# A diffusion block on one core: tokens turned early and kept in SBUF, and another order of the first loads

## The reference, cut to what matters

```python
mod   = silu(c)     @ ada_w[i] + ada_b[i]        # 2048 -> 6 * 2048
sh1, sc1, g1, sh2, sc2, g2 = split(mod, 6)
mod_c = silu(c_ctx) @ ada_w[i] + ada_b[i]
csh1, csc1, ... = split(mod_c, 6)
h  = rms_norm(x,   norm1_g[i]) * (1 + sc1)  + sh1
hc = rms_norm(ctx, norm1_g[i]) * (1 + csc1) + csh1
proj = h @ w_in[i]                               # and hc @ w_in[i][:, :N_QKV]
```

## Time and profile before

| | us |
|---|---|
| median of 3 runs | 1719.82 |
| the profiled execution | 1720.02 |
| its span | 1718.3 |
| TensorE busy in it | 1677.8 (98%) |
| VectorE busy | 1086.3 (63%) |
| ScalarE busy | 752.6 (44%) |
| chain that ended last: TensorE, DMA, VectorE | 94%, 3%, 1% |

### The profile page before, as it was taken

The page is one execution under the profiler, slowest core; times in us unless marked ns, Lnnn a source line. Parts: engine busy times, 40 slices in busy tenths (PEclk is TensorE's granted clock), DMA queues, the critical chain, the costliest instruction groups (busy, mean ns, idle before and its releaser), DMA issues.

```text
span 1718.3 us, 23725 instructions
## 1 busy us (share of the span) xinstructions
PE 1677.8 (98%) x8768; PEld 1371.5 (80%) x8768; DVE 1086.3 (63%) x1366; ACT 752.6 (44%) x962; POOL 108.6 (6%) x161
## 2 busy tenths in 40 slices
PE   4999999999999999999999999999999999999997
PEld 1568888888888678888888788888888888888886
DVE  1338787768887674554555666666666666655556
ACT  2233321623222664444444555555555555544444
POOL 0002222122121000000000000000000000000000
PEclk7999999999999999999999999999999999999999
DMA  9999888269896128566565566666666665655552
GB/s 353 386 387 347 298 296 297 79 215 328 259 321 200 52 90 271 191 189 191 192 234 195 148 190 190 188 191 188 191 187 191 185 184 188 202 195 194 191 193 83
DMA packets 161813, 371.47 MB, mean 216 GB/s; under 512 B 11671, under 2 KB 12423, under 8 KB 160598
## 3 DMA queue, kind: packets, MB, share of 16 engines
q1 hardware_dynamic: 140240, 291.65, 52.5%
q0 software_dynamic: 20144, 74.22, 12.7%
q10 hardware_dynamic: 1366, 4.74, 0.7%
HBM read 368.36 MB, written 2.21 MB: 216 GB/s over the span
## 4 chain that ended last, share of the span: by engine, by line
PE 94%; DMA 3%; DVE 1%; issue 0%; ACT 0%; SPq 0%; DVEq 0%; POOL 0%; ACTq 0%
PE ps L1885 21%; PE ps L1884 11%; PE ps L1899 10%; PE ps L1901 10%; PE ps L1900 10%; PE ps L2253 5%; PE ps L2252 5%; PE ps L2254 5%; PE ps L1811 4%; PE ps L1813 3%; PE ps L1812 3%; DMA raw<-in_ada_w 3%; PE ps L1882 1%; PE ps L1803 1%; PE ps L1968 1%; PE ps L1950 1%
## 5 line engine op out<-in xcount | busy, mean ns | idle before, releaser
L1147 DVE TENSOR_TENSOR w_lo<-raw,w_hi 128x1024 fp32r<-128x1024 f32 x480 | 584.5, 1223 | 419.7 <-ACT w_hi L680 419.2
L680 ACT CAST w_hi<-raw 128x1024 fp32r<-128x1024 f32 x480 | 503.4, 1050 | 763.3 <-PE ps L1885 271.2
L1885 PE MATMUL ps<-h2T,w_hi 128*128 128x512 f32 x1320 | 462.7, 394 | 0.0
L1884 PE MATMUL ps<-h2T,w_lo 128*128 128x256 f32 x1320 | 366.8, 278 | 0.0
L1885 PEld LDWEIGHTS ps<-h2T,w_hi 128*128 128x128 f32 x1320 | 247.8, 188 | 53.7
L1884 PEld LDWEIGHTS ps<-h2T,w_lo 128*128 128x128 f32 x1320 | 248.2, 188 | 3.9
L1899 PE MATMUL ps<-w_hi,hT 128*128 128x512 f32 x512 | 201.7, 394 | 0.0
L1901 PE MATMUL ps<-w_hi,hT 128*128 128x512 f32 x512 | 199.4, 389 | 0.0
L1900 PE MATMUL ps<-w_lo,hT 128*128 128x512 f32 x512 | 199.3, 389 | 0.0
L1222 DVE SCALAR_TENSOR_TENSOR ada_acc<-ada_raw,silu_c,ada_acc 128x512 f32<-128x512 f32 x240 | 179.9, 750 | 29.4 <-DMA ada_raw<-in_ada_w 14.1
L603 POOL DMA_DIRECT2D ada_raw<-in_ada_w x128 | 91.2, 712 | 381.5 <-DVE ada_acc L1222 226.4
(11 more groups left out here) (231 smaller groups left out, 1985.6 us busy)
## 6 DMA issues: line engine op xcount, KB each, us to landing
raw<-in_ffn_w_up SPq DMA_DIRECT2D x176, 512.0 KB, 3.8
raw<-in_w_in SPq DMA_DIRECT2D x152, 512.0 KB, 4.8
ada_raw<-in_ada_w POOLq DMA_DIRECT2D x128, 512.0 KB, 5.9
raw<-in_ffn_w_down SPq DMA_DIRECT2D x88, 512.0 KB, 4.3
raw<-in_ada_w SPq DMA_DIRECT2D x64, 512.0 KB, 10.4
raw<-in_w_out SPq DMA_DIRECT2D x32, 512.0 KB, 4.4
raw<-in_w_branch_a SPq DMA_DIRECT2D x16, 512.0 KB, 3.6
raw<-in_w_branch_b SPq DMA_DIRECT2D x16, 512.0 KB, 3.6
```

Source lines behind the costliest of these rows:

```text
L680: act.copy(w_hi[:, s % SPLIT_SLOTS, :], raw[:, s, :]).then_inc(hi_ready[s], 1)
L1147: dve.tensor_tensor(w_lo[:, s % SPLIT_SLOTS, :], raw[:, s, :], w_hi[:, s % SPLIT_SLOTS, :], ALU.subtract).then_inc(lo_ready[s], 1)
L1884: pe.matmul(ps[:, b + t, 0:SEQ], w_lo[:, row4(s), at], high(kc), start=False, stop=False)
L1885: return pe.matmul(o, w_hi[:, row4(s), at], both(kc), start=False, stop=(kc == KC - 1))
```

## The change

- SP requests units 0 and 1 first, and the identity, `c` and `c_ctx` behind them. ACT requests the tokens first and the eight small loads of parameter rows behind them.
- The tokens are turned in 16 parts: part n holds channels of two kc for the two tiles of one stream, parts 0 to 7 for `x`, 8 to 15 for `ctx`. They stand behind units 3 to 11 of the first quarter (`TURN_AFTER`), in four PSUM banks. VectorE copies 7 and ScalarE 9 of them into `turned`, which lies where the low part of `hT` will lie. The modulation reads `turned` and waits for all copies once.
- TensorE turns the parameter rows behind unit 6 of the first quarter instead of ahead of all units. `turn_mod(0)` stands behind unit 15 instead of behind unit 17.
- VectorE's list: lambda first, then the scaling of `x`, three copies of turned parts, the parameter rows, the scaling of `ctx`, the other four copies. ScalarE copies its nine parts behind the second stream's root.
- K0 to K5 are requested earlier by 3 or 4 units, most of their tiles stand up to 4 units earlier, and three tiles of K5 stand behind the last unit instead of two. A first tile of a K waits for each of its two channels by itself.
- Two semaphores (`ones_ready`, `lam_ready`) are gone.

```diff
-K_AFTER = (3, 10)
-K_TILES = {(0, 0): (1, 6), (0, 1): (1, 8), (0, 2): (1, 10), (0, 3): (1, 12),
-           (1, 0): (1, 13), (1, 1): (1, 15), (1, 2): (2, 1), (1, 3): (2, 3),
-           (2, 0): (2, 6), (2, 1): (2, 8), (2, 2): (2, 10), (2, 3): (2, 12),
-           (3, 0): (2, 13), (3, 1): (2, 15), (3, 2): (3, 1), (3, 3): (3, 3),
-           (4, 0): (3, 5), (4, 1): (3, 6), (4, 2): (3, 8), (4, 3): (3, 9),
-           (5, 0): (3, 11), (5, 1): (3, 12), (5, 2): (3, 15), (5, 3): (3, 15)}
+K_AFTER = (0, 6)
+K_TILES = {(0, 0): (1, 3), (0, 1): (1, 5), (0, 2): (1, 6), (0, 3): (1, 8),
+           (1, 0): (1, 10), (1, 1): (1, 12), (1, 2): (1, 15), (1, 3): (2, 1),
+           (2, 0): (2, 4), (2, 1): (2, 5), (2, 2): (2, 7), (2, 3): (2, 8),
+           (3, 0): (2, 10), (3, 1): (2, 12), (3, 2): (2, 15), (3, 3): (3, 1),
+           (4, 0): (3, 4), (4, 1): (3, 5), (4, 2): (3, 7), (4, 3): (3, 9),
+           (5, 0): (3, 11), (5, 1): (3, 15), (5, 2): (3, 15), (5, 3): (3, 15)}
+TURN_PARTS = KC
+TURN_BANKS = (7, 1, 6, 5)
+TURN_AFTER = {3: (0, 1), 4: (2, 3), 5: (4, 5), 6: (6,), 7: (7,), 8: (8, 9), 9: (10, 11), 10: (12, 13), 11: (14, 15)}
+TURNS_OF_VECTOR = (0, 1, 2, 8, 10, 12, 14)
+TURNS_OF_SCALAR = tuple(n for n in range(TURN_PARTS) if n not in TURNS_OF_VECTOR)
...
     hT = place("hT", lat, [P, 2, 2, KC, SEQ], F32R)
+    turned = place("turned", lat, [P, 2, 2, KC, SEQ])
...
+        def turned_part(n):
+            st, pair = divmod(n, KC // 2)
+            return turned[:, st, 1, 2 * pair:2 * pair + 2, :].rearrange("p k n -> p (k n)")
+        def part_kept(n):
+            if n in TURNS_OF_VECTOR:
+                return kept_by_vector, TURNS_OF_VECTOR.index(n) + 1
+            return kept_by_scalar, TURNS_OF_SCALAR.index(n) + 1
...
-            sp.dma_start(ident, constants[:, C_IDENT:C_IDENT + P]).then_inc(rows_landed, 16)
-            sp.dma_start(param_rows[0:16, 0, :], c.rearrange("a (k p) -> (a k) p", p=P)).then_inc(rows_landed, 16)
-            sp.dma_start(param_rows[16:32, 0, :], c_ctx.rearrange("(k p) -> k p", p=P)).then_inc(rows_landed, 16)
...
                     n = KC * q + kc
+                    if n == 2:
+                        sp.dma_start(ident, constants[:, C_IDENT:C_IDENT + P]).then_inc(rows_landed, 16)
+                        sp.dma_start(param_rows[0:16, 0, :], c.rearrange("a (k p) -> (a k) p", p=P))\
+                            .then_inc(rows_landed, 16)
+                        sp.dma_start(param_rows[16:32, 0, :], c_ctx.rearrange("(k p) -> k p", p=P))\
+                            .then_inc(rows_landed, 16)
...
+            act.dma_start(tokens[:, 0:TOK, :], x[0].rearrange("(t p) n -> p t n", p=P)).then_inc(tokens_landed, 16)
+            act.dma_start(tokens[:, TOK:2 * TOK, :], ctx[0].rearrange("(t p) n -> p t n", p=P))\
+                .then_inc(ctx_landed, 16)
             act.dma_start(param_rows[0:96, 1, :], by_row(ada_b)).then_inc(rows2_landed, 16)
...
-                act.wait_ge(tokens_turned, kc + 1)
+                if kc == 0:
+                    act.wait_ge(kept_by_vector, len(TURNS_OF_VECTOR))
+                    act.wait_ge(kept_by_scalar, len(TURNS_OF_SCALAR))
...
-                    act.activation(modulated[:, kc % 4, st, :], ps[:, turn_bank(kc), st * SEQ:(st + 1) * SEQ],
+                    act.activation(modulated[:, kc % 4, st, :], turned[:, st, 1, kc, :],
...
                 root1(st)
+            for n in TURNS_OF_SCALAR:
+                act.wait_ge(tokens_turned, n + 1)
+                act.copy(turned_part(n), ps[:, TURN_BANKS[n % 4], :]).then_inc(kept_by_scalar, 1)
...
+            def keep_turned(n):
+                dve.wait_ge(tokens_turned, n + 1)
+                dve.tensor_copy(turned_part(n), ps[:, TURN_BANKS[n % 4], :]).then_inc(kept_by_vector, 1)
...
             mean_square1(0)
             inverse_root1(0)
             norm_tokens(0)
             norm_tokens(1)
+            keep_turned(0)
+            keep_turned(1)
+            keep_turned(2)
+            dve.wait_ge(vecs_turned, 2)
...
             mean_square1(1)
             inverse_root1(1)
             norm_tokens(2)
             norm_tokens(3)
+            for n in TURNS_OF_VECTOR[3:]:
+                keep_turned(n)
...
+            def turn_tokens(n):
+                st, pair = divmod(n, KC // 2)
+                if pair == 0:
+                    pe.wait_ge(normed1, TOK * (st + 1))
+                if n >= 4:
+                    pe.wait_ge(*part_kept(n - 4))
+                for i in range(2):
+                    kc = 2 * pair + i
+                    for t in range(TOK):
+                        mm = pe.transpose(ps[:, TURN_BANKS[n % 4], (2 * i + t) * P:(2 * i + t + 1) * P],
+                                          tokens[:, 2 * st + t, kc * P:(kc + 1) * P], ident)
                 mm.then_inc(tokens_turned, 1)
...
             for _, q, kc in ADA_UNITS:
                 unit_ada(q, kc)
-                if (q, kc) == (1, 1):
-                    turn_mod(0)
+                if (q, kc) == (0, 6):
+                    turn_vectors()
+                if q == 0:
+                    for n in TURN_AFTER.get(kc, ()):
+                        turn_tokens(n)
+                    if kc == KC - 1:
+                        turn_mod(0)
...
-                        if (s, t) in ((1, 1), (3, 1), (5, 2)):
+                        if (s, t) in ((1, 2), (3, 2), (5, 1)):
                             turn_mod(q)
-                if kc == 14:
-                    turn_tokens(SHARE * q)
-                if q and kc in (2, 4, 5):
-                    turn_tokens(SHARE * (q - 1) + {2: 1, 4: 2, 5: 3}[kc])
-            turn_tokens(KC - 3)
```

More of the change, by code:

```diff
@@ L728, in _ @@
             act.dma_start(param_rows[2 * FF_TILES:2 * FF_TILES + 1, 5, :], diff_norm_g).then_inc(rows2_landed, 16)
[L729 to L732, removed]
+            act.wait_ge(start_dve, 1)
             warm_up(ACT.Exp)
@@ L1162, in step @@
                 dve.wait_ge(start_dve, steps)
-            dve.memset(ones[:], 1.0).then_inc(ones_ready, 1)
+            step(dve.memset(ones[:], 1.0))
             step(dve.memset(epsilon[:], EPS))
@@ L1278, in _ @@
             norm_tokens(1)
+            keep_turned(0)
+            keep_turned(1)
+            keep_turned(2)
+            dve.wait_ge(vecs_turned, 2)
+            dve.tensor_copy(vecs[:, 2 * KC:512], ps[:, 3, 2 * KC:512]).then_inc(vecs_ready, 1)
+            dve.tensor_copy(vecs[:, 512:513], ps[:, 2, 88:89]).then_inc(vecs_ready, 1)
+            dve.wait_ge(vecs_ready, 3)
+            dve.tensor_scalar(dng[:], vecs[:, V_DNG:V_DNG + 1], 1.0 - LAMBDA_INIT, None, ALU.mult)\
+                .then_inc(vecs_ready, 1)
             mean_square1(1)
@@ L1767, in _ @@
             pe.wait_ge(c_ready, 1)
-            pe.wait_ge(ones_ready, 1)
-            def turn_tokens(kc):
-                if kc == 0:
-                    pe.wait_ge(normed1, 2 * TOK)
-                if kc >= 2:
-                    pe.wait_ge(modulated_ready, 2 * (kc - 1))
-                if kc % SHARE == 1:
-                    pe.wait_ge(mod1_ready, kc // SHARE + 1)
-                for t in range(2 * TOK):
-                    mm = pe.transpose(ps[:, turn_bank(kc), t * P:(t + 1) * P], tokens[:, t, kc * P:(kc + 1) * P],
-                                      ident)
+            def turn_tokens(n):
[9 more added lines that the diff above has]
+                                          tokens[:, 2 * st + t, kc * P:(kc + 1) * P], ident)
                 mm.then_inc(tokens_turned, 1)
@@ L1786, in turn_mod @@
                 if q:
-                    pe.wait_ge(modulated_ready, 2 * SHARE * q)
+                    pe.wait_ge(mod1_ready, q)
+                else:
+                    pe.wait_ge(kept_by_vector, len(TURNS_OF_VECTOR))
+                    pe.wait_ge(kept_by_scalar, len(TURNS_OF_SCALAR))
                 rows = PIECE_AT[-1] + 2
@@ L1813, in products_k, with unit_k @@
                 return pe.matmul(o, w_lo[:, row4(slot), at], hT[:, :, 0, kc, :], start=False, stop=(kc == KC - 1))
-            def unit_k(s, slot, t, b):
+            def unit_k(s, slot, t, b, head=False):
                 for i in range(2):
+                    if head and t == 0:
+                        pe.wait_ge(hT_ready, 2 * s + i + 1)
                     mm = products_k(slot, t, b, 2 * s + i, i)
@@ L1823, in head_k, with turn_vectors @@
                 if t == 0:
-                    pe.wait_ge(hT_ready, 2 * s + 2)
                     take(0, s)
-                mm = unit_k(s, s, t, 0)
+                mm = unit_k(s, s, t, 0, head=True)
                 if t == TILES - 1:
                     mm.then_inc(used[s], 1)
-            pe.wait_ge(rows2_landed, 128)
-            pe.wait_ge(vecs_ready, 1)
-            pe.transpose(ps[:, 3, V_ADAB:V_ADAB + P], param_rows[:, 1, :], ident)
-            for tap in range(TAPS):
-                pe.transpose(ps[:, 3, V_CONV + 88 * tap:V_CONV + 88 * (tap + 1)], param_rows[0:88, 2 + tap, :],
-                             consts[0:88, 0:88])
```

(17 more changed lines are left out.)

15 lines of the change are left out of this document (3 added, 12 removed).

## The result

The changed kernel took 1725.67 us (median of 16 runs) against 1720.08 us: ratio 1.0031, 95% interval 1.0025 to 1.0038, 4.3 to 6.5 us slower. Forecast were 1718.7 us, 1716.2 to 1723.4. One of the 16 runs took 5002 us with TensorE slow throughout and happens to be the profiled one; the ratio leaves it out, and all that follows reads another execution of the same kernel (1726.59 us, span 1724.9), which is the experiment `after_again`.

A forecast was written before the change was run, and what follows sets the result against it. The head, ending when job 1 starts (131.87 us), was taken as bound by DMA transfer, with TensorE 1.77 us behind at u63. u63 0.4 earlier and 0.7 off the tail gave -1.1: 1718.7 us, range 1716.2 to 1723.4.

The forecast's parts named there:

- c behind two units: Head, SP's queue: at 4.9 us a unit beside tokens, u1 lands at 12.1 and c about 12.6.
- rival D: Head: tokens crowd out the units, c 3.0 us later, DMA loss 5.2; +1.9, 1721.7 us; chance 0.08.
- What hangs on c: Head, behind c's landing: units start at 14.5, ScalarE squares x from 16.5, x can be turned from 23.8.
- What that does to the loads: Head, unit loads: u12 frees u20's slot at 45.5, not 43.3, so the DMA loses 2.2 us; bounds 0 to 9.3.
- the budget: Head, unit loads: u19 lands at 45.2; u20 must be asked for some 1.9 us before that, by 43.3.
- B: Head, turning: clock stays at 1.2 GHz through the parts; every part low +6.0, 1725.8 us; chance 0.13.
- C: Tail: clock falls around u60 to u63, tiles behind u63 cost 1.4 to 2.4 us more; 1720.1 to 1721.1; chance 0.11.
- E: End of the head: TensorE is not freed, u63 still runs 1.77 us behind its landing; 1720.5 us; chance 0.02.
- The tail: From u63 to job 1: 0.7 us goes with the two parts there; bounds 0.4 to 1.5.
- The start of the DMA: Fifth and sixth us: large loads requested first fill 0.75 us of empty DMA time; 0.8 us won, bounds 0 and 1.2.
- lateness: At u63: the 1.77 us that TensorE stood behind its data go, since nine parts fewer lie in the middle.
- rival A: Head: the loads never starve; -0.8 - 1.77 - 0.7 = -3.3, 1716.5 us, or 1716.1 with the fuller start; chance 0.16.

The follow-up runs named there:

- tokens_2k: The changed kernel with x and ctx each loaded in four strips of 512 columns, so in 2 KB pieces: 1725.09 us, ratio 1.0042.
- c_first: The changed kernel with one edit undone, identity, c and c_ctx requested ahead of unit 0 again: 1717.59 us, ratio 0.9983.
- squares_first: The changed kernel with x squared and scaled ahead of the work on c: 1718.28 us, ratio 0.9992.
- c_first_again: The changed kernel with identity, c and c_ctx ahead of unit 0, run once more: 1716.30 us, ratio 0.9985.
- order_back: The changed kernel with both orders of loads as before (c ahead of units, parameter rows ahead of tokens), the turning still changed: 1719.36 us, ratio 0.9993.

## Why the prediction was wrong, step by step

**The step that failed is "c behind two units": "I take 4.9. Then u1 lands at 2.3 + 9.8 = 12.1 and c about 12.6".** It lies between a mean over u3 and u4 (5.45) and one over five units (4.4), and both mixed times: u0 and u1 of the kernel before had mostly landed before the tokens came, and u4 came as they ended: from 6 to 9 us ScalarE's queue carried 0.09 MB of rows, SyncE's 1.01. The one row wholly inside, u3's 6.4, stood in the text and was given to rival D. Measured: u0 landed at 11.47, 10.6 behind its request; u1 at 17.81, 6.3 later; c_ctx at 20.48, 2.7 behind u1 where 0.5 was allowed. The sum is 7.9 us late. D was the right mechanism, still too cheap by 4.9: it kept the 0.5 behind u1, charged u0 as 6.4 from 2.3 on, and nothing for 6 to 9 us, when the three queues together moved 0.65 MB and GpSimd's took 53.0% of the engines' time:

```profile
q0 software_dynamic: 48, 0.13, 53.0%
q10 hardware_dynamic: 51, 0.42, 36.4%
q1 hardware_dynamic: 50, 0.10, 10.8%
```

The Trainium skill, "DMA: Bandwidth & Descriptors", Queues, rings and completion order, has the engines go round the queues packet by packet. The trace agrees (132 packets against 131), and the estimate made from it, 6.8 a unit, was nearer to the measured 6.3 than the value taken. `tokens_2k` tests it by size: equal packets, equal shares.

**What hangs on c was right.** From c_ctx to the first part 11.2 us were forecast and 11.4 measured. With c 7.9 late, the part came at 31.9 in place of 23.8. `c_first` has the first part at 23.81, where the prediction had it, and took 1717.59 us where 1718.7 were forecast.

**What that does to the loads: the mechanism held, the size came from the step before and from one more term.** Forecast loss 2.2, measured 8.2. u12 ended, and u20 was asked for, at 49.55 in place of 45.5, so 4.0 later. That is c's 7.9 and some 0.2 behind it, less 4.1, since the turning was quicker than charged: from the first part to u12's end 17.6 us (31.90 to 49.5) in place of 21.7, at the full clock for most of it, eight transposes and a unit in 1.59:

```profile
44.07 0.64 PE L1837 MATMUL ps<-raw,c_pair 128*32 128x256 f32 x8
44.64 1.09 PE L1810 MATMUL ps<-consts,tokens 128*128 128x128 f32 x8
45.66 0.64 PE L1837 MATMUL ps<-raw,c_pair 128*32 128x256 f32 x8
```

u4 landed at 25.09 in place of 23.3, which puts u20's turn 1.8 later. And the budget had u20 land 3.3 behind its request, 1.9 as for a lone small load and 1.37 for the unit itself; it took 6.3, 3.0 more:

```profile
L550 SPq DMA_DIRECT2D raw<-in_ada_w x1: 368/368/368, 49.5 to 49.5; - x1
...
DMA to landing us min/median/max: 6.3/6.3/6.3
```

2.2 + 4.0 - 1.8 + 3.0 = 7.4, as measured: u20 landed at 55.82, and on the pace it would have been 25.09 + 17 x 1.37 = 48.4. The last 0.8 was lost at the key load behind u21. `squares_first` shows the same term alone: there no load between u4 and u20 came late, u20 was asked for at 43.28, 1.9 ahead of the budget's 45.2, and landed 6.5 later, 1.9 behind its turn. Why a unit takes so long there is open. In the changed kernel the engines had run dry before, from u12 on (u12 landed 4.20 behind u11, u13 3.45 behind u12), behind u4's wait, for which the prediction had no term: 5.8 of the 8.2 were lost when u19 landed, at 52.83, and u20 ran up the rest. With c in time the errors of size nearly offset one another: in `c_first` u20 was asked for 4.2 earlier than forecast (41.33), took 2.8 longer (6.1) and had its turn 0.8 later, 2.2 - 4.2 + 2.8 - 0.8 = 0, and 0.2 was lost.

**B is refuted, though its time, 1725.8, is the one that was measured.** That is chance: the loss has another cause. Only the first parts ran at half clock (0.55 over 28 to 35 us); then it was granted in full in the midst of parts and units: 0.97 over 35 to 42 us, with TensorE busy 6.22 of 7.00, and 1.00 from 28 to 42 in `c_first`. By the rule of the Trainium skill, "TensorE: Matmul & The Clock Gate", Part 4, that transposes don't count as busy in the same way, the parts should have stayed at half; the trace doesn't show that, though units stand between the parts and the runs don't part the two.

**C and E are refuted.** Behind u60 to u63 the clock is full in the changed kernel, and u63 waits for its data, as its row above shows:

```profile
118.00:126.00 8.00, 6.57 (x52) 3.86 (x51) 1.33 (x4) 2.32 (x4) 0.64 (x1) 1.00 1.06 389
```

**The tail** gave 0.9 for 0.7 forecast, in every changed kernel whose u63 is on time.

**The start of the DMA did come and was given back.** us 5 and 6 of the changed kernel (answers to the earlier trace rows):

```profile
4.00:5.00 1.00, 0.00 (x0) 0.00 (x0) 0.00 (x0) 0.00 (x0) 0.00 (x0) 1.00 0.92 371
5.00:6.00 1.00, 0.00 (x0) 0.00 (x0) 0.00 (x0) 0.00 (x0) 0.00 (x0) 1.00 1.03 379
```

But 7 to 21 us run at 361 and 383 GB/s in place of 397 and 417, and by 21 us both kernels have moved 6.65 MB. "It has something to carry" was right, "the small rows' own time is only moved back" too; the step from there to 0.8 us won was not, since the time they take later is the time won. -0.8 measured as 0 in `c_first` (u4 at 24.09 against 24.06) and as +1.0 in the changed kernel.

So the sum becomes: u4 +1.0, loss +8.2, lateness -1.7, tail -0.9: +6.6, which is job 1's shift. For `c_first`: 0, +0.2, -1.7, -0.9: -2.4, as measured; that is rival A less its start of the DMA.

## What to carry to other kernels

A small load that a whole chain waits for goes ahead of large ones on its queue; here it waited their full time behind them, and beside a queue with longer rows that time was set by the sizes of the packets, to be read from the queues' packets and bytes in a window of a few us. How far ahead a load must be asked for is read from loads of its own size with others under way (6.3 us here), not from a lone small one (1.9). Ask not only how late an operand becomes but what else queues behind its consumer on the same engine: here the token norm stood behind c on ScalarE for no reason of data, and taking it ahead won back 6.8 of the 9.1 us that c first won, with c as late as ever. The best version is the changed kernel with c first: 2.4 to 3.2 us off job 1, ratio 0.9983 (0.9974 to 0.9992) and 0.9985 (0.9976 to 0.9994).

## What the runs showed that was not expected

**The same kernel, at half clock for longer or shorter, far behind the change.** Between 970 and 988 us the granted clock fell for 6.8 us in some executions, for 3.4 or not at all in others; first `c_first`, then `c_first_again`, one kernel:

```profile
970.00:976.00 6.00, 3.58 (x16) 2.70 (x15) 4.77 (x15) 3.20 (x8) 0.00 (x0) 0.72 0.23 80
976.00:982.00 6.00, 6.00 (x29) 5.21 (x29) 5.93 (x10) 4.72 (x9) 0.00 (x0) 0.71 0.41 109
```

```profile
970.00:976.00 6.00, 4.30 (x19) 3.53 (x20) 4.81 (x14) 4.13 (x9) 0.00 (x0) 0.72 0.11 43
976.00:982.00 6.00, 6.00 (x39) 5.31 (x38) 5.90 (x10) 4.75 (x9) 0.00 (x0) 1.00 0.59 170
```

From job 1 to the end of the span it is 1586.8 us in `c_first` and 1586.4 in `after_again` and in the kernel before, all with 6.8 us at half clock there; 1585.3 in `c_first_again`, with 3.4; 1584.8 in `squares_first` and 1584.7 in `order_back`, with none. So some 1.7 us lie in a stretch that no edit here touches, while the best version wins 2.4 to 3.0 us by the medians. Why the clock falls for longer in one execution than in the next was not tried. For a change in the head, the start of job 1 is the sharper measure.

**A 128 KB load that fills 128 partitions cost the DMA engines about 1 us on either queue**: the 0.44 and 0.37 MB that were missing in its 2 us take 1.1 and 1.0 us at 387 GB/s, and come on top of the 0.34 us for its own bytes.
